# Norms between the stages of a decoder trunk taken by halves of 288 tokens

## The reference

```
h = x + 0.5 * rms(ffn(rms(x)))            # ffn1: silu(n @ w_gate) * (n @ w_up) @ w_down, 4096 wide
z = rms(h) @ w_in -> u, v, a, gate        # 512 columns each
A = u * (tril(W_s) @ layer_norm(v) + b_s) # in chunks of 128 tokens
B = silu(layer_norm(causal_dwconv(a * sigmoid(gate), 31 taps)))
h = h + rms([A | B] @ w_out)
h = h + rms(attend(rms(h) @ w_q, k, v) @ w_o)   # 4 heads of 256, 256 memory tokens
y = h + 0.5 * rms(ffn2(rms(h)))
```

## Time and profile before

| | |
|---|---|
| median of 3 runs | 1705.68 us (1703.89 to 1707.11) |
| the profiled execution | 1702.72 us, its span 1701.0 us |
| TensorE busy | 1603.9 us, 94% of the span |
| VectorE busy | 1027.5 us, 60% |
| ScalarE busy | 699.6 us, 41% |
| mean granted TensorE clock | 0.974 of full speed |

### The profile page before, as it was taken

How to read it: one execution, slowest core, us unless ns; L and a number is a source line. 1 busy time by engine, 2 the same in 40 slices (tenths; PEclk the granted TensorE clock), 3 DMA queues, 4 the chain that set the end, 5 groups by cost and what they waited for, 6 DMA issues and landing times.

```text
span 1701.0 us, 28434 instructions
## 1 busy us (share of the span) xinstructions
PE 1603.9 (94%) x11770; PEld 1550.1 (91%) x11770; DVE 1027.5 (60%) x1310; ACT 699.6 (41%) x1204; POOL 203.5 (12%) x177
## 2 busy tenths in 40 slices
PE   6999999999999979997989999799999999999997
PEld 6899999999999979996978869689999999999996
DVE  4773675476467467998345442677367547646744
ACT  5451353254145354641443333445135325414532
POOL 2020120121022000004001010002012012102200
PEclk8999999999999989999999999899999999999997
DMA  4222233233223322222334452122223323322321
GB/s 145 75 86 88 75 100 100 76 100 100 75 79 97 124 83 69 90 82 93 124 104 149 149 176 82 41 75 88 87 75 100 100 76 99 100 75 76 100 75 56
DMA packets 137903, 159.16 MB, mean 94 GB/s; under 512 B 3197, under 2 KB 130769, under 8 KB 137768
## 3 DMA queue, kind: packets, MB, share of 16 engines
q1 hardware_dynamic: 132192, 138.16, 25.6%
q0 software_dynamic: 5488, 19.10, 3.2%
q10 hardware_dynamic: 96, 0.02, 0.0%
HBM read 152.22 MB, written 5.40 MB: 93 GB/s over the span
## 4 chain that ended last, share of the span: by engine, by line
PE 82%; DVE 12%; ACT 3%; issue 1%; DMA 0%; POOL 0%; ACTq 0%; DVEq 0%; POOLq 0%
PE slot L1771 40%; PE slot L1895 36%; DVE f L1581 4%; DVE wp L1210 1%; PE slot L1815 1%; ACT wp L692 1%; DVE f L1246 1%; PE slot L1799 1%; PE slot L2119 1%; DVE f L1588 1%; DVE h L1250 1%; PE slot L2138 1%; PE slot L1829 1%; DVE f L1290 1%; DVE folded L1225 1%
## 5 line engine op out<-in xcount | busy, mean ns | idle before, releaser
L1895 PE MATMUL slot<-nb,wu 128*128 128x288 f32 x4704 | 632.7, 295 | 10.6 <-issue 5.9
L1895 PEld LDWEIGHTS slot<-nb,wu 128*128 128x128 f32 x4704 | 628.4, 188 | 12.9 <-issue 8.1
L1771 PE MATMUL slot<-mid,wp 128*128 128x288 f32 x4176 | 573.6, 298 | 26.5 <-DVE wp L1210 15.1
L1771 PEld LDWEIGHTS slot<-mid,wp 128*128 128x128 f32 x4176 | 564.7, 191 | 32.3 <-issue 24.8
L692 ACT ACTIVATE wp<-raw 128x1024 fp32r<-128x1024 f32 x120 | 127.0, 1059 | 364.3 <-PE slot L1771 340.8
L1210 DVE TENSOR_TENSOR wp<-raw,wp 128x1024 fp32r<-128x1024 f32 x120 | 146.9, 1224 | 139.5 <-ACT wp L692 139.4
L610 POOL TENSOR_TENSOR raw<-raw,q 128x512 f32<-128x512 f32 x56 | 80.2, 1431 | 872.3 <-DVE wu L1346 559.9
L1771 PE MATMUL slot<-n,wp 128*128 128x288 f32 x1152 | 165.6, 304 | 12.4 <-DVE n L1232 11.9
L1771 PEld LDWEIGHTS slot<-n,wp 128*128 128x128 f32 x1152 | 159.7, 195 | 16.8 <-issue 14.4
L1474 DVE TENSOR_TENSOR f<-slot,f 128x576 f32<-128x576 f32 x48 | 36.3, 756 | 135.3 <-PE slot L1771 135.3
L1351 DVE TENSOR_TENSOR wu<-q,wu 128x1024 fp32r<-128x1024 f32 x56 | 88.0, 1572 | 24.6 <-ACT wu L807 23.4
(11 more groups left out here) (246 smaller groups left out, 1432.3 us busy)
## 6 DMA issues: line engine op xcount, KB each, us to landing
raw<-in_ffn_w_gate_dram SPq DMA_DIRECT2D x32, 1024.0 KB, 5.4
raw<-in_ffn_w_up_dram SPq DMA_DIRECT2D x32, 1024.0 KB, 5.4
raw<-in_ffn_w_down_dram SPq DMA_DIRECT2D x32, 1024.0 KB, 4.9
raw<-in_mix_w_in_dram SPq DMA_DIRECT2D x8, 1024.0 KB, 5.3
kring<-in_cache_mem_k_dram POOLq DMA_DIRECT2D x6, 1024.0 KB, 5.7
raw<-in_xattn_w_k_dram SPq DMA_DIRECT2D x4, 1024.0 KB, 4.9
raw<-in_xattn_w_v_dram SPq DMA_DIRECT2D x4, 1024.0 KB, 5.0
raw<-in_mix_w_out_dram SPq DMA_DIRECT2D x4, 1024.0 KB, 5.0
```

Of the source, the lines that this page charges most:

```text
L1771: ins = pe.matmul(slot(u)[:, half, 0:HALF], wp[:, J % 2, wi, kt], X(xi, kt, half), start=kt == 0 and k == 0, stop=kt == KT - 1 and k == le ...
L1895: ins = pe.matmul(dst[:, 0:HALF], wu[:, p, wi, kt], nb[:, p, xi, kt], start=start and kt == 0 and k == 0, stop=kt == KH - 1 and k == len(P ...
```

## The change

1. **Halves.** Every norm works on 288 tokens at a time. TensorE's `last_pair` starts the last two jobs of a stage together: half 0 of both, half 1 of the first, with the sum and the spread of half 0's root between, half 1 of the second. `first_four` does half 0 of the next stage's first two jobs tile by tile, jobs 2 and 3 follow three tiles (`LAG`) behind; then half 1. Ahead of ffn1, where no post-norm is, it does the four sums and the spread of half 0 first, then the products. The sums use free banks of the jobs' own slots, so the auxiliary uses `pre*` and `post*` go out of the plan.
2. **Weights.** The first two jobs of each such stage (and the fifth) have buffers of their own in free regions, `X0` and `X1`, so their weights are prepared before the last pair. For q these lie where the sample keys b=2 and b=1 are loaded; POOL's loads of b=1 and b=2 now wait for q jobs 1 and 4.
3. **Turns.** The memory tokens are turned behind glu0 and the state rows, the memory values and convolution rows ahead of `out`.
4. **FFN loop.** TensorE's hardware loop covers blocks 1 and 2; block 3 is written out.
5. **Tail.** The output tiles of tokens 0 to 255 are turned after half 0, the others after half 1, with the samples' inside the same loop.
6. **Taps innermost.** `taps` is [sample, token, tap] in place of [tap, sample and token].
7. **LayerNorm of v.** VectorE applies it in two operations with gain and offset; POOL's two go.
8. ScalarE does the SiLUs of the convolution part ahead of its copies of the first two v4 jobs.

```diff
-                with pe.Fori(1, BLOCKS) as b:
+                with pe.Fori(1, BLOCKS - 1) as b:
                     block_of(0, b)
+                block_of(0, BLOCKS - 1)
```

```diff
+            def last_pair(name, i, post, X, b=0):
+                a, z = start_job(name, i, b), start_job(name, i + 1, b)
+                for J, u in (a, z):
+                    for kt in range(KT):
+                        half_products(J, u, X, kt, 0, half_done)
+                for kt in range(KT // 2):
+                    half_products(*a, X, kt, 1, job_done)
+                sum_squares(post, 0)
+                for kt in range(KT // 2, KT):
+                    half_products(*a, X, kt, 1, job_done)
+                spread_half(post, 0)
+                for kt in range(KT):
+                    half_products(*z, X, kt, 1, job_done)
```

```diff
+            def sum_squares(post, half):
+                wait_slot(pe, sum_place(post, half)[0])
+                pe.wait_ge(*normed_to(post, "added", KT - 3))
+                fold_in(sum_bank(post, half), FOLD_H, acc[:, cols(half)], True, False)
+                for e in range(2):
+                    pe.wait_ge(*normed_to(post, "squared", KT - 2 + 2 * half + e + 1))
+                    ins = fold_in(sum_bank(post, half), FOLD_H, sq[:, e, cols(half)], False, e == 1)
+                ins.then_inc(sum_done, 1)
```

`first_four`, the branch behind a post-norm:

```diff
+                    for t in range(KT + LAG):
+                        if t < KT:
+                            pe.wait_ge(*normed_to(pre, "ready", t + 1))
+                            if t == 0:
+                                start(0)
+                            both(0, t, 0)
+                        if t >= 2 and t % 2 == 0 and t <= KT:
+                            sum_pair(pre, 0, t // 2 - 1)
+                        if t == 1:
+                            sum_squares(post, 1)
+                        if t == 3:
+                            spread_half(post, 1)
+                        if t >= LAG:
+                            if t == LAG:
+                                start(2)
+                            both(2, t - LAG, 0)
...
+                for t in range(KT):
+                    pe.wait_ge(*normed_to(pre, "ready", KT + t + 1))
+                    both(0, t, 1)
+                    if post and t == 0:
+                        spread_half(pre, 0)
+                    if post and t >= 3 and t % 2 == 1:
+                        sum_pair(pre, 1, (t - 3) // 2)
...
+                for t in range(KT):
+                    both(2, t, 1)
+                    if post and t == 0:
+                        sum_pair(pre, 1, KT // 2 - 1)
+                    if post and t == 3:
+                        spread_half(pre, 1)
```

The order on ScalarE and on VectorE (`last` is the last pair's tile by half):

```diff
+            def normed_pair(post, pre, g, job, last, kinds, dst):        # ScalarE
+                for e in range(2):
+                    last(e, 0)
+                root(post, D, kinds[0], 0)
+                last(0, 1)
+                prepare(J0 + 2)
+                take_root(post, 0)
+                norm_half(post, pre, g, 0, {1: [lambda: last(1, 1)], 2: [lambda: root(post, D, kinds[0], 1)],
+                                            3: [lambda: prepare(J0 + 3)], 4: [lambda: take_root(post, 1)]}, dst)
+                norm_half(post, pre, g, 1, {2: [lambda: root(pre, D, kinds[1], 0)], 4: [lambda: take_root(pre, 0)]}, dst)
+                prepare(J0 + 4)
+                root(pre, D, kinds[1], 1)
+                take_root(pre, 1)
...
+            def normed_pair(post, g, pre, gpre, job, dst, first, last=None):  # VectorE
+                reciprocal(post, 0)
+                if last:
+                    last(0, 1)
+                prepare(J0 + 2)
+                norm_half(post, g, pre, gpre, 0, {2: [lambda: last(1, 1)] if last else [],
+                                                  4: [lambda: reciprocal(post, 1)], 5: [lambda: prepare(J0 + 3)]}, dst)
+                norm_half(post, g, pre, gpre, 1, {4: [lambda: reciprocal(pre, 0)], 6: [lambda: take_half(job, first, 0)]}, dst)
+                prepare(J0 + 4)
+                reciprocal(pre, 1)
+                take_half(job, first, 1)
```

POOL, and ScalarE's loop over the q jobs:

```diff
             for b in range(NB):
-                if b < 3:
+                if b == 0:
                     pool.wait_ge(job_done, pl.base["out"][0] + 1)
+                elif b == 1:
+                    pool.wait_ge(job_done, pl.base["q"][0] + 2)
+                elif b == 2:
+                    pool.wait_ge(job_done, pl.base["q"][0] + 5)
...
             act.wait_ge(qs_zero, 1)
             for t in range(KT):
-                if t:
+                if t >= 3:
                     prepare(pl.base["q"][0] + t + 2)
```

Taps and LayerNorm:

```diff
-                    V.tensor_reduce(f[:, 4 + ct, SEQ:T], taps[ct % 2][:, :, :].rearrange("p k n -> p n k"), AX_X, ALU.add)\
+                    V.tensor_reduce(f[:, 4 + ct, SEQ:T], taps[ct % 2][:, :, :, :].rearrange("p b k n -> p (b k) n"), AX_X, ALU.add)\
...
+                    V.scalar_tensor_tensor(out=sv[0:m, i], in0=sv[0:m, i], scalar=bag[0:m, 2 * i:2 * i + 1], in1=lng[0:m, :],
+                                           op0=ALU.subtract, op1=ALU.mult).then_inc(sv_n, 1)
...
+                    V.scalar_tensor_tensor(out=sv[0:m, i], in0=sv[0:m, i], scalar=vrs[0:m, i:i + 1], in1=lnb[0:m, :],
+                                           op0=ALU.mult, op1=ALU.add).then_inc(sv_b, 1)
```

More of the change, by code:

```diff
@@ L296, in build @@
         sums = {}
-        for s, parts in (("pre", ("squared", "recip", "added", "summed", "hi", "ready")),
-                         ("post", ("squared", "recip", "added", "scaled", "done"))):
+        for s, parts in (("pre", ("squared", "added", "summed", "hi", "ready")),
+                         ("post", ("squared", "added", "scaled", "done"))):
             made = {x: sem(f"{s}_{x}") for x in parts}
@@ L1244, in post_norm, with norm_half @@
+                    V.tensor_tensor(acc[:, cols((half + pair) % 2 if half else 0)], sq[:, 0, c], sq[:, 1, c], ALU.add)\
+                        .then_inc(sums[pre]["added"], 1)
+            def norm_half(post, g, pre, gpre, half, beside, dst=None):
+                c = cols(half)
+                if post:
+                    dve.wait_ge(taken, taken_no(post, half))
                 for t in range(KT + 2):
-                    if t < KT:
-                        V.scalar_tensor_tensor(out=f[:, t], in0=f[:, t], scalar=gain[g][t], in1=R[:, :],
+                    for step in beside.get(t, ()):
+                        step()
+                    if post and t < KT:
+                        V.scalar_tensor_tensor(out=f[:, t, c], in0=f[:, t, c], scalar=gain[g][t], in1=R[:, c],
@@ L1503, in ffn @@
                 groups(0, last)
-                for i in range(KT):
+                for i in range(KT - 2):
                     take_down(i, last)
@@ L1880, in ffn @@
+            def ffn(name, before, pre, post):
                 J0, u0 = pl.base[name]
@@ L1976, in block_of @@
                     down_part(*second, range(6, 8))
-                    for i in range(2, KT):
+                    last = isinstance(b, int) and b == BLOCKS - 1
+                    for i in range(2, KT - 2 if last else KT):
                         job(name, 16 + i, half_of(mid), b=b)
-                jobs_normed(name, pre, 4, mid)
+                    if last:
+                        last_pair(name, 16 + KT - 2, post, half_of(mid), b)
+                first_four(name, before, pre, half_of(mid))
                 pe.wait_ge(b_lo, 8 * STAGE[name] + 4)
@@ L2003, in _ @@
             turn("spatial", [(eight(aux("spatial"))[:, hd, :], wsr[:, hd, :]) for hd in range(4)])
-            ffn("ffn1", "pre1")
-            sum_squares("post1")
+            ffn("ffn1", None, "pre1", "post1")
+            first_four("glu0", "post1", "pre2", half_of(n))
+            pe.wait_ge(ld_st, 16)
+            for r in range(2):
+                turn(f"state{r}", [(eight(aux(f"state{r}"))[:, ct, 0:120], straw[:, r, ct * P:(ct + 1) * P]) for ct in range(CT)])
             for t in range(MT):
@@ L2009, in _ @@
                 turn(f"mem{t}", [(eight(aux(f"mem{t}"))[:, kt, :], memraw[:, t, kt * P:(kt + 1) * P]) for kt in range(KT)])
-            jobs_normed("glu0", "pre2", 4)
-            pe.wait_ge(ld_st, 16)
-            for r in range(2):
-                turn(f"state{r}", [(eight(aux(f"state{r}"))[:, ct, 0:120], straw[:, r, ct * P:(ct + 1) * P]) for ct in range(CT)])
             jobs("glu1", half_of(n), None, 4)
@@ L2090, in _ @@
             turn("glus", [(aux("glus")[0:NB * DEC, 0, ct * P:(ct + 1) * P], gsm[:, ct, :]) for ct in range(CT)])
-            jobs_normed("q", "pre3", KT)
+            jobs("out", half_of(mid), lambda kt: pe.wait_ge(mid_ready, MID0["mix"] + kt + 1), KT - 2)
+            last_pair("out", KT - 2, "post2", half_of(mid))
+            first_four("q", "post2", "pre3", half_of(n))
+            for i in range(4, KT):
+                job("q", i, half_of(n))
             for e in range(4):
```

617 lines of the change are left out of this document (402 added, 215 removed).

## The result

| | before | after |
|---|---|---|
| median | 1704.8 us (1702.1 to 1707.6) | 1711.7 us (1710.0 to 1714.9) |
| ratio, 95% interval | | 1.0042 (1.003 to 1.0053) |
| profiled execution | 1702.72 us, span 1701.0 | 1712.75 us, span 1711.0 |
| mean granted TensorE clock | 0.974 | 0.976 |

The forecast was 1695.5 us: faster. The kernel is 0.4% slower. Each ratio is certain to about 0.0013, so such a difference to about 3 us. The two profiled executions differ by 10.0 us where the medians differ by 6.9; readings of places in a trace speak of the profiled executions.

The account below looks back on a forecast made before the run. TensorE was taken as the bound, waiting for VectorE at norms and for weights. Terms -2.9 + 4.6 + 1.0 + 1.9 - 2.1 - 2.7 - 9.7 = -9.9 gave 1695.5 us; own range 1689 to 1702, 8 in 10 of all 1684 to 1706.

Parts of the forecast that it names:

- the convolution: Convolution: shorter VectorE reduces and LayerNorm work remove nearly all of TensorE's 7.6 us wait at its end: -9.7 us.
- the memset's stall: Ahead of q job 5: ScalarE waits for POOL's memset of `qs` behind q job 4, so TensorE stands 6.8 us.
- The loop: TensorE's FFN hardware loop loses its last turn, one back edge less in each FFN: -2.7 us, at worst 0.
- VectorE's last pair sum of half 0 waits for a fold of TensorE's (21.7): Norm ahead of glu0: VectorE's half 0 ends at 21.7 us from the old last job's end; half 1 takes 11.7 more.
- and 2 lost to the clock: Norm ahead of glu0: 2 us of low clock counted in TensorE's 26.4 us, after sparse tiles.
- rival (a): The clock holds through the sparse tiles: 2 us less at three norms and 2 at ffn2's job 4, 1687.5; chance 0.16.
- Pair starts at -10.4. ... Both halves 0 done at -4.0: Last pair: after a 2.4 us stand for weights, both first halves take 6.4 us; VectorE starts the post-norm at 2.9.
- Ahead of ffn1: Start of ffn1: first four jobs wait until half 0 is normed, summed and spread: +1.9 us, bounds -1 and +5.
- Later than 45 us after the point 0: Sign that the forecast is wrong: four jobs end later than 45 us after the old last job's end.
- (b): Ahead of q job 5: the wait for the memset isn't there, 8.6 us less, 1687; chance 0.10.
- (c): Convolution: VectorE's reduces don't shorten, TensorE keeps 5.7 us of its wait and 1.8 of low clock: 1703; chance 0.10.
- (d): Norm halves: handing tiles between engines sets the pace, 0.45 us a step, seven halves 12.6 us more: 1708; chance 0.14.

Follow-up runs that it names:

- e1: The kernel before with one edit, taps innermost: 1697.4 us, 0.9946 of before.
- e3: The changed kernel with POOL's load of keys b=3 and memset of `qs` ahead of the loads b=1 and b=2: 1703.2 us, 0.9991 of before.
- e4: The changed kernel with the last pair's second job started, with its wait, behind the first job's half 0: 1698.0 us, 0.9954 of before.
- e9: The changed kernel, order kept, with 20 and 6 extra matmuls ahead of the third and fourth tile at three norms: 1703.2 us, 0.9990 of before.
- e6: The changed kernel with the post-norm's second spread ahead of the third tile's products and pair sums alternating between halves of `acc`: 1699.3 us, 0.9973 of before.
- e12: The changed kernel, waits kept, with 20 small matmuls filling TensorE's wait ahead of each last pair: 1707.6 us, 1.0023 of before.
- e10: The changed kernel with three edits ahead of ffn1: TensorE's spread, VectorE's second reciprocal and `take_half` moved: 1705.5 us, 1.0012 of before.
- e8: The changed kernel with the edits of e3, e4 and e6, and ffn1's spread behind two tiles: 1677.0 us, 0.9849 of before.
- e11: e8 plus e10's edits in both FFNs, takes and gates behind operand parts, job 4 beginning with the tiles ready first: 1669.0 us, 0.9791 of before.
- the mended kernel: The kernel of e11, 1669.0 us; with filler matmuls added where TensorE waits it measured 1669.7 us, 0.9799 of before.

## Why the prediction was wrong

- **Right, with their sizes:** the convolution (reduce 2.2 us; wait 0.88; -9.2 against -9.7, and e1), the wait of 2.4 on `wp` at four pairs (2.56 each), the memset's stall (6.88 against 6.8; e3), the wait of 8 us ahead of ffn2 (8.31), the turns, the tail. The loop gave more than was said in this profile; TensorE's time through the blocks of ffn1 is 478.0 us in it, 479.8 in e4's with the same code and 480.9 before, so part of it is scatter.
- **"VectorE's last pair sum of half 0 waits for a fold of TensorE's (21.7)".** This is the step that failed, at three norms: half 1 began at 27.0, 24.2 and 26.7. The working has 17.0 without this wait (2.9, 10.8, 0.6, 1.2, 1.5), so it priced the waits of half 0 behind the root's as one of 4.7 us. There are three: for ScalarE's high part (3.21 us, behind `take_root` and TensorE's spread) and twice for TensorE's folds behind the products of jobs 2 and 3 (1.18 and 2.32), 6.7 together ahead of glu0 and 5.9 ahead of q. What was missing is the clock: this work of TensorE runs at the low level, and with the clock kept (e9) half 0 lasts 18.9 us ahead of q and ffn2, the forecast's 18.8. The order is why VectorE waits at these three places: with it mended they are gone and half 0 lasts 15.0 (e6). The filler gave back 8.9 us, the mended order 11.8.
- **"and 2 lost to the clock".** The forecast had a price for the clock, but on the wrong path: the 2 us stand in TensorE's sum of 26.4, while 41.4 is added up from VectorE's 21.7 and 11.7 and what stands behind them. So they are not in the forecast of q job 4, and rival (a) could not have taken them off it at the three norms. From there on, q job 4 came 21.4 us behind the start of half 1 where the sum has 19.7; it is 21.4 in e9 too, so this 1.7 isn't the clock, and which term it belongs to is open.
- **"Pair starts at -10.4. ... Both halves 0 done at -4.0".** The wait was priced, the clock that can fall behind it wasn't, though the same forecast did so behind the memset's stall. Ahead of glu0 and ffn2 the pair's first 60 matmuls took 1.4 us more (9.58 and 9.60 against 8.15) and VectorE started 4.7 and 4.5 us behind the point 0; ahead of q they didn't, and it started at 3.1 where 2.9 was said. The whole edit's price was 15 us and not 10 (e4); filling the wait returned 3.2 of it (e12).
- **Ahead of ffn1,** "3.3 of folds, spreads and one wait": VectorE's queue was left out (its `take_half` waited 5.51 us, its reciprocal stood behind eight operations): 5.4 us and not 1.9, beyond the bound of 5 by 0.4 (e10 gave back 5.1).
- **Its own sign.** "Later than 45 us after the point 0" for four jobs came true: 48.4 ahead of glu0, 45.6 ahead of q.
- **Slips.** 1705.68 less 9.9 is 1695.8, not 1695.5. Glu1 at 45.4 against 48.5 is -3.1, not -2.9. 3.47 less 2.2 is 1.3 a reduce, not the 1.4 that it used; the four took 3.47 to 3.75. Job 3's 8.08 less 6.4 is 1.7, not 1.8. None of them changes the outcome.
- **Rivals.** (a) and (b) didn't happen. (c) is refuted by e1. (d) came out as to the time, 1708 against 1711.7, but by luck, not by its mechanism: VectorE's steps are 0.37 and 0.43 us (621.11 to 621.48; 621.84 to 622.27) where 0.37 and 0.40 were forecast, not 0.45. Its first clause, that handing tiles between the engines sets the pace, was the true one; its test, the length of a step, looked in the wrong place. The Trainium skill ("VectorE: DVE Perf Modes", "The TRN2 errata") gives each small tile a fixed cost. The trace agrees: eight three-operand operations take 3.52 us on 288 columns (44.84) and 5.93 on 576, so two halves cost 1.1 us more. But the forecast had this in it (21.6 against 19.5), so it does not explain the miss.
- **Range.** 1684 to 1706 left out an error that repeats: three norms have the same order, so their errors add (6.5, 4.2 and 6.4 us of the 19.9 between -9.9 and +10.0), and four pairs have the same stand.

## What to carry to other kernels

When a norm is cut in halves, write down for each engine what stands ahead of each hand-over; counting one engine's operations misses the waits that cross (here 6.7 of 22 us), and what the others do in that time may run at the low clock. Put the price of the clock on the path that ends last. Start a job only ahead of its own first product, and put small reductions and spreads into a gap that TensorE has anyway. Price a stand of TensorE as its wait plus slow work that may follow (1.3 to 1.6 us behind 18 of 28 stands of 2.56 us here). Filler matmuls can tell the two apart, but taking the wait away was worth far more (15.0 against 3.2 us), and in the mended kernel fillers gave nothing.

## What the runs showed of the hardware

- Around the end of a stand of 2.56 us ahead of a pair (605.26) the granted clock was 0.75, 0.50 and 0.90 in the stretches of 2 us from 604, 606 and 608. The same stand ahead of q left it at 1.00, and so did the one ahead of glu0 in e3; the work behind it was slow at 18 of 28 places in seven profiles. With small matmuls in the stand it was slow at none of four (e12).
- The mean granted clock of the same stretch differs between kernels that do the same work there: 1.00 in e8 and 0.87 in e11 ahead of glu0, where the norm took 35.6 and 38.0 us. A gain of 2 us in one norm of one profile is within that.
- A float32 reduce of 31 x 64 elements took 3.47 to 3.75 us with the 31 summed ones 256 bytes apart, and 2.20 to 2.22 us with them side by side. The Trainium skill ("VectorE: DVE Perf Modes", "Mode 1× (REGULAR)") says that this mode takes any strides, at one result a cycle; the runs disagree as to the pace with this stride.
